# Banded local attention: the third and fourth group's query projections moved behind the value products and cut into runs of three or four parts

## The chip, the cores and the metric
The kernel runs on one core of one Trainium2 chip. The metric is the device time of one execution in microseconds (us); lower is better. The core has five engines that run their own instruction streams and meet only at semaphores: TensorE (PE: matrix products and transposes; PEld is its weight load), VectorE (DVE), ScalarE (ACT), GpSimd (POOL) and SyncE (SP, which issues the transfers).

## The reference
Four layers are computed on x of shape (1, 512, 1024) in float32. The change lies in the attention of the last but one part of the second block:

```python
q = (rmsnorm(h, b_pre_norm) @ b_w_q).reshape(bsz, s, 16, 64)      # 16 heads of 64
q = partial_rotary(q, cos, sin)
attn = sliding_window_sink_attention(q, k_sh, v_sh, b_sinks) @ b_w_o
# per block of 128 queries: keys of this block and of the one before, window 128
scores = jnp.where(valid, q @ k.T / 8, NEG)
probs = softmax(concat([scores, sink]))[..., :-1]
out = probs @ v
```

The 16 query heads share 4 key/value heads: 4 groups of 4 heads (KVH = 4, GROUP = 4), and the sequence has T = 4 blocks of 128, so there are 16 units of attention (UNITS), unit n being group g = n // 4 and block b = n % 4.

## The kernel before, in words
Every large product runs as three float32 products of a high and a low half (`mm3`, lines 1820 to 1822). The weights of each stage arrive in two buffers; ScalarE makes the high half (`split_high`, L743), GpSimd the low half (`low`, L639).

**The projection.** `queries(g, first, last)` projects the hidden state of all 512 tokens onto group g's 256 query columns: 16 parts of 3 matmuls each (two output tiles m, eight depths k), into PSUM banks 0 and 1. A call with `first == 0` waits for the split weights and for `q2_sin` of the group before last; the last part signals `used[g % 2]`. The group's result then goes: ScalarE copies it to `q2raw` (`raw_queries`, L1107), TensorE makes the partner rows (`partners`, L2324), VectorE multiplies them by the sine (L1802, signals `q2_sin`), GpSimd multiplies `q2raw` by the cosine (L627) and adds both (L630).

**A unit.** Unit n's work is spread over three engines:
- TensorE: `score2(n)` (4 heads, L2337), later `turn2(n)` (transposes of the probabilities, L2347; 4 or 8), later `weigh2(n)` (times the values, L2359; 4 or 8).
- VectorE: `top2(n)` (L1773 to L1778: window, maximum, sink), signals `m2_ready`; after ScalarE's exponentials `norm2(n)` (L1784 to L1787: sum, reciprocal, normalisation of the probabilities), signals `p2_ready`.
- ScalarE: `weigh2(n)` (exponentials, L1114 and L1116) and `turned2(n)` (transposed probabilities out of PSUM, L1125), `p2T_ready`.

`score2(n)` waits for `m2_ready` of unit n - 1. `turn2(n)` waits for `p2_ready` of unit n, that is for `norm2(n)`. VectorE's order in loop pass n is `top2(n + 1)`, in the passes with b == 1 the sine product of the next group and (from the second group on) `low_out` of the last one (L1791), and then `norm2(n)`.

**The order on TensorE** is written out by hand. The projections of groups 0 and 1 come ahead of the loop over the 16 units; those of groups 2 and 3 fill the units of groups 0 and 1. In loop pass n TensorE issues `score2(n + 2)`, a projection run in the passes with b == 1, `turn2(n)`, `weigh2(n - 1)`, and a projection run in the passes with b == 2 and 3. Each engine executes in order, so a wait in front of `turn2` holds all that follows.

After the 16 units come the output projection (`out_stage("wo")`) and the last feed-forward layer (`in_stage("gu1")`, `out_stage("dn1")`).

Of the kernel before, what the change touches and what calls it, by code (L numbers as in the profile page):

```python
# [17 lines left out]
K = D // P  # L18
# [17 lines left out]
HD, KVH, GROUP = 64, 4, 4  # L36
# [155 lines left out]
def program(nc, a, out):  # L192
    with ExitStack() as ctx:
# [1621 lines left out]
        def _(pe):  # L1815
            mm, tr = nc.tensor.matmul, nc.tensor.transpose

            def mm3(dst, lh, ll, rh, rl, first, last):

                mm(dst, lh, rh, start=first, stop=False, skip_group_check=True)  # L1820
                mm(dst, lh, rl, start=False, stop=False, skip_group_check=True)  # L1821
                return mm(dst, ll, rh, start=False, stop=last, skip_group_check=True)  # L1822

            def wcols(w, s):
                return w[s][:, :].rearrange("p (k n) -> p k n", n=256)
# [235 lines left out]
            for f in range(K):  # L2061
                g, m = f // 2, f % 2
# [243 lines left out]
            def queries(g, first, last, tok=slice(0, S)):  # L2306

                s = g % 2
                if first == 0:
                    pe.wait_ge(w_split[s], B.split[s] + g // 2 + 1)  # L2310
                    if g >= 2:
                        pe.wait_ge(q2_sin, g - 1)
                for j in range(first, last):
                    m, k = j // K, j % K
                    c = slice(m * P, (m + 1) * P)
                    ins = mm3(PS[:, m, tok], wcols(WH, s)[:, k, c], wcols(WL, s)[:, k, c], hH[:, k, tok], hL[:, k, tok], k == 0, k == K - 1)
                if last == 2 * K and tok.stop == S:
                    ins.then_inc(used[s], 1)

            def partners(g):  # L2320

                pe.wait_ge(q2_raw, g + 1)
                for m in range(2):
                    ins = mm(PS[:, m if g else 6 + m, :], turn_b, q2raw[:, m, :], start=True, stop=True)  # L2324
                ins.then_inc(q2_turn, 1)

            def score2(n):
                g, b = n // T, n % T
                if b == 0:
                    pe.wait_ge(q2_ready, g + 1)  # L2330
                if n:
                    pe.wait_ge(m2_ready, n)
                lo = max(b - 1, 0) * P
                for h in range(GROUP):
                    r = slice((h % 2) * HD, (h % 2 + 1) * HD)
                    c = (h // 2) * 2 * P
                    ins = mm(PS[:, 2 + h % 2, c + (0 if b else P):c + 2 * P], q2[g % 2][r, h // 2, b * P:(b + 1) * P],  # L2337
                             kdup[r, g, lo:(b + 1) * P], start=True, stop=True)
                ins.then_inc(s2_done, 1)

            def turn2(n):
                if n:
                    pe.wait_ge(p2T_ready, n)
                pe.wait_ge(p2_ready, n + 1)
                for h in range(GROUP):
                    for k in range(0 if n % T else 1, 2):
                        ins = tr(two(4)[:, 2 * h + k, :], p2[n % 3][:, h, k * P:(k + 1) * P], ident)  # L2347
                ins.then_inc(t2_done, 1)

            def weigh2(n):  # L2350
                g, b = n // T, n % T
                if b == 0 and g:
                    pe.wait_ge(o2_low, 2 * g)
                pe.wait_ge(p2T_ready, n + 1)
                ks = range(0 if b else 1, 2)
                c = (b % 2) * 2 * P
                for k in ks:
                    for o in range(2):
                        ins = mm(PS[o * HD:(o + 1) * HD, 6 + b // 2, c:c + 2 * P], vall[:, b - 1 + k, g * HD:(g + 1) * HD],  # L2359
                                 p2T[n % 2][:, 4 * o + k:4 * o + 4:2, :], start=(k == ks[0]), stop=(k == 1), skip_group_check=True)  # L2360
                ins.then_inc(pv2_done, 1)
# [13 lines left out]
            def ahead_wo(first, last):  # L2375

                for kt in range(first, last):
                    s, d = kt // 2, kt % 2
                    pe.wait_ge(w_split[s], BASE["wo"].split[s] + 1)
                    pe.wait_ge(o2_low, kt + 1)  # L2380
                    pe.wait_ge(q2_sin, KVH - 1)
                    out_tile(o2H, o2L, kt, s, d, 0, kt == 0, False)

            AHEAD = {UNITS - 3: (0, 1), UNITS - 2: (1, 2), UNITS - 1: (2, 4)}
            for n in range(UNITS):
                g, b = n // T, n % T
                if n + 2 < UNITS:
                    score2(n + 2)
                if n in AHEAD:
                    ahead_wo(*AHEAD[n])  # L2390
                if b == 0 and g + 1 < KVH:
                    partners(g + 1)
                if b == 1 and g + 2 < KVH:
                    queries(g + 2, 0, 5)
                turn2(n)
                if n:
                    weigh2(n - 1)
                if b >= 2 and g + 2 < KVH:
                    queries(g + 2, *((5, 10), (10, 2 * K))[b - 2])
            weigh2(UNITS - 1)  # L2400
            turn = turner("wo", 4, x_hat)
            out_stage("wo", o2H, o2L, lambda kt: pe.wait_ge(o2_low, kt + 1),
# [39 lines left out]
```

## Time and profile before

| | us |
|---|---|
| median of 3 runs | 1876.33 |
| lowest and highest of them | 1875.57, 1877.78 |
| the profiled execution, its own time | 1876.41 |
| its span (first to last instruction) | 1874.3 |
| TensorE busy | 1807.3 (96% of the span), 8798 matmuls |
| VectorE busy | 791.5 (42%) |
| ScalarE busy | 746.1 (40%) |
| GpSimd busy | 788.9 (42%) |

Times in the trace are microseconds from the start of the span. The 16 units and the projections in them lie at about 1359 to 1463 us. A row of the timeline is one instruction, or several alike merged (x8), with its start, its duration, and in brackets the idle time of the engine just before it and whose signal ended it. Matmuls overlap, so the time that a piece of work takes on TensorE is read from its start to the next start. The table by stretches gives the busy time of every engine and PEclk, the share of full clock granted to TensorE (1.00 is 2.4 GHz, 0.50 is 1.2 GHz).

### The profile page before, as it was taken

How to read it: one execution, taken by the hardware profiler on the slowest of the kernel's cores; microseconds unless marked ns; L12 is line 12 of the kernel's file. 1: busy time of each engine (PE TensorE's matmuls, PEld its weight loads, DVE VectorE, ACT ScalarE, POOL GpSimd, SP SyncE). 2: the span in 40 equal slices, each digit the busy share in tenths (PEclk: the TensorE clock that was granted, in tenths of full speed). 3: DMA queues.
4: the chain of work that ended last, by engine and by line, in shares of the span. 5: the costliest groups of instructions: out<-in, count | busy, mean ns of one | idle time of the engine just before them, and what ended most of it. 6: DMA issues, size and time to landing. Idle time of an engine off the chain costs nothing.

```text
span 1874.3 us, 24002 instructions
## 1 busy us (share of the span) xinstructions
PE 1807.3 (96%) x8798; PEld 1494.8 (80%) x8798; DVE 791.5 (42%) x1388; ACT 746.1 (40%) x1043; POOL 788.9 (42%) x992
## 2 busy tenths in 40 slices
PE   6999999989999999899999999999997999999998
PEld 6788878878788878788888888888965788888886
DVE  5775775367677632623241111103678341111102
ACT  3423331365656542322253344214456453443212
POOL 0375454354101162355335555443443135555351
PEclk9999999999999999999999999999999999999999
DMA  9543565221212132233233343232311133433321
GB/s 314 172 135 90 151 202 183 93 82 37 73 36 73 45 124 90 68 93 132 90 91 90 93 109 112 102 112 82 114 45 45 46 91 90 109 92 90 120 94 67
DMA packets 209320, 190.94 MB, mean 102 GB/s; under 512 B 10475, under 2 KB 189538, under 8 KB 209250
## 3 DMA queue, kind: packets, MB, share of 16 engines
q1 hardware_dynamic: 208608, 189.69, 32.7%
q8 instruction: 46, 0.75, 0.2%
q10 hardware_dynamic: 642, 0.29, 0.1%
q14 instruction: 24, 0.20, 0.0%
HBM read 187.86 MB, written 2.10 MB: 101 GB/s over the span
## 4 chain that ended last, share of the span: by engine, by line
PE 86%; DVE 5%; ACT 3%; POOL 3%; issue 2%; DMA 0%; SPq 0%; ACTq 0%; POOLq 0%; DVEq 0%
PE PS L1820 27%; PE PS L1822 26%; PE PS L1821 26%; POOL w_low L639 2%; PE PS L2168 1%; ACT w_high L743 1%; PE PS L1949 1%; PE PS L2199 1%; POOL w_low L677 1%; DMA ada_raw<-in_ada_w 0%; DVE soft L1775 0%; DVE probs L1773 0%; PE PS L2359 0%; PE PS L2191 0%; PE PS L2190 0%
## 5 line engine op out<-in xcount | busy, mean ns | idle before, releaser
L639 POOL TENSOR_TENSOR w_low<-w_raw,w_high 128x256 fp32r<-128x256 f32 x905 | 701.6, 811 | 841.2 <-ACT w_high L743 841.2
L1820 PE MATMUL PS<-h_high,w_high 128*128 128x512 f32 (+1 forms) x1488 | 560.7, 377 | 15.4 <-DVE h_low L1453 7.0
L1821 PE MATMUL PS<-h_low,w_high 128*128 128x512 f32 (+1 forms) x1488 | 553.7, 372 | 0.0
L1822 PE MATMUL PS<-h_high,w_low 128*128 128x512 f32 (+1 forms) x1488 | 553.6, 372 | 0.0
L743 ACT ACTIVATE w_high<-w_raw 128x2048 fp32r<-128x2048 f32 (+2 forms) x150 | 280.2, 1868 | 683.8 <-PE PS L1822 669.1
L1820 PEld LDWEIGHTS PS<-h_high,w_high 128*128 128x128 f32 x1488 | 281.6, 189 | 68.6 <-DVE h_low L1453 8.3
L1822 PEld LDWEIGHTS PS<-h_high,w_low 128*128 128x128 f32 x1488 | 281.5, 189 | 48.8
L1821 PEld LDWEIGHTS PS<-h_low,w_high 128*128 128x128 f32 x1488 | 281.8, 189 | 45.7 <-issue 0.7
L1363 DVE TENSOR_TENSOR gate_buf<-gate_buf,PS 128x512 f32<-128x512 f32 x44 | 30.3, 688 | 334.9 <-ACT gate_buf L876 334.3
L1183 DVE TENSOR_TENSOR w_low<-w_raw,w_high 128x2048 fp32r<-128x2048 f32 (+1 forms) x15 | 33.3, 2220 | 325.4 <-ACT w_high L743 325.4
L1820 PE MATMUL PS<-w_high,ff_high 128*128 128x512 f32 x352 | 137.2, 390 | 0.1
L1822 PE MATMUL PS<-w_high,ff_low 128*128 128x512 f32 x352 | 137.0, 389 | 0.0
L1821 PE MATMUL PS<-w_low,ff_high 128*128 128x512 f32 x352 | 137.0, 389 | 0.0
L667 POOL TENSOR_TENSOR w_low<-w_raw,w_high 128x256 fp32r<-128x256 f32 x35 | 29.8, 882 | 165.0 <-ACT w_high L743 165.0
L1820 PEld LDWEIGHTS PS<-w_high,ff_high 128*128 128x128 f32 x352 | 66.1, 188 | 14.6 <-POOL w_low L639 1.0
L1821 PEld LDWEIGHTS PS<-w_low,ff_high 128*128 128x128 f32 x352 | 66.1, 188 | 13.7
L1822 PEld LDWEIGHTS PS<-w_high,ff_low 128*128 128x128 f32 x352 | 66.1, 188 | 13.6
L1820 PE MATMUL PS<-w_high,o_high 128*128 128x512 f32 x192 | 75.5, 393 | 0.6 <-POOL w_low L639 0.6
L1821 PE MATMUL PS<-w_low,o_high 128*128 128x512 f32 x192 | 74.8, 389 | 0.0
L1822 PE MATMUL PS<-w_high,o_low 128*128 128x512 f32 x192 | 74.8, 389 | 0.0
L977 ACT ACTIVATE probs<-PS,soft 128x128 f32<-128x128 f32 (+1 forms) x64 | 33.8, 528 | 75.8 <-DVE soft L1573 75.8
L1367 DVE TENSOR_TENSOR ff_low<-gate_buf,ff_high 128x512 f32 x44 | 41.9, 953 | 40.8 <-ACT ff_high L880 40.8
(310 smaller groups left out, 2574.8 us busy)
## 6 DMA issues: line engine op xcount, KB each, us to landing
w_raw<-in_f_gate_up SPq DMA_DIRECT2D x88, 512.0 KB, 4.9
w_raw<-in_f_down SPq DMA_DIRECT2D x40, 512.0 KB, 4.3
w_raw<-in_e_w_in SPq DMA_DIRECT2D x32, 512.0 KB, 5.0
gains<-in_ada_w SPq DMA_DIRECT2D x16, 1024.0 KB, 5.2
w_raw<-in_a_w_in SPq DMA_DIRECT2D x24, 512.0 KB, 4.5
w_raw<-in_o_w_in SPq DMA_DIRECT2D x20, 512.0 KB, 4.3
ada_raw<-in_ada_w SPq DMA_DIRECT2D x8, 1024.0 KB, 13.3
w_raw<-in_e_w_out SPq DMA_DIRECT2D x16, 512.0 KB, 5.6
```

The costliest lines, as they stand in the source:

```text
L639: ins = nc.gpsimd.tensor_tensor(WL[s][:, piece], raw[s][:, piece], WH[s][:, piece].bitcast(F32), ALU.subtract)
L667: ins = nc.gpsimd.tensor_tensor(WL[1][:, piece], raw[1][:, piece], WH[1][:, piece].bitcast(F32), ALU.subtract)
L677: nc.gpsimd.tensor_tensor(WL[1][:, h:], raw[1][:, h:], WH[1][:, h:].bitcast(F32), ALU.subtract).then_inc(pool_half, 1)
L743: nact(WH[s][:, 0:n], raw[s][:, 0:n], ACT.Copy).then_inc(w_high[s], 1)
L977: nact(pm[u % 2][:, 0:w], PS[:, 2 + u % 2, 0:w], ACT.Exp, scale=MLA_SCALE, bias=soft[:, u % 2, 1, 0:1], accum_out=soft[:, u % 2, 2, 0:1]). ...
L1183: v.tensor_tensor(WL[s][:, 0:size], raw[s][:, 0:size], WH[s][:, 0:size].bitcast(F32), ALU.subtract).then_inc(w_split[s], 1)
L1363: v.tensor_tensor(buf[s][:, :], buf[s][:, :], PS[:, 2 * s + 1, :], ALU.mult).then_inc(prod_ready, 1)
L1367: v.tensor_tensor(lows[:, f, :], buf[s][:, :], fH[:, f, :].bitcast(F32), ALU.subtract).then_inc(gate_low, 1)
L1820: mm(dst, lh, rh, start=first, stop=False, skip_group_check=True)
L1821: mm(dst, lh, rl, start=False, stop=False, skip_group_check=True)
L1822: return mm(dst, ll, rh, start=False, stop=last, skip_group_check=True)
L1949: ins = tr(two(2 * t if b is None else b)[:, k, :], src[:, k * P:(k + 1) * P], ident)
```

## The change
The projections of groups 2 and 3 are the same 16 parts each, in the same order, in the same passes of the loop. Only where they stand in a pass, and the length of the runs, differ:

| pass | before | after |
|---|---|---|
| b = 1 | `queries(0, 5)`, `turn2`, `weigh2` | `turn2`, `weigh2`, `queries(0, 4)` |
| b = 2 | `turn2`, `weigh2`, `queries(5, 10)` | `queries(4, 7)`, `turn2`, `weigh2`, `queries(7, 10)` |
| b = 3 | `turn2`, `weigh2`, `queries(10, 16)` | `queries(10, 13)`, `turn2`, `weigh2`, `queries(13, 16)` |

```diff
                 if b == 0 and g + 1 < KVH:
                     partners(g + 1)
-                if b == 1 and g + 2 < KVH:
-                    queries(g + 2, 0, 5)
+                if b >= 2 and g + 2 < KVH:
+                    queries(g + 2, *((4, 7), (10, 13))[b - 2])
                 turn2(n)
                 if n:
                     weigh2(n - 1)
-                if b >= 2 and g + 2 < KVH:
-                    queries(g + 2, *((5, 10), (10, 2 * K))[b - 2])
+                if b and g + 2 < KVH:
+                    queries(g + 2, *((0, 4), (7, 10), (13, 2 * K))[b - 1])
             weigh2(UNITS - 1)
```

No instruction is added or removed, and no transfer is touched.

## Rows read from the trace of the kernel before

**Rows 1.** Who TensorE waited for, 1500 us to the end: total us, times, longest.
```profile
PE PS L1820 <- DVE h_low L1453: 0.7, 1, 0.7
```

**Rows 2.** Timeline of TensorE, units 1 to 3 (start us, us, engine line op).
```profile
1372.11 1.14 PE L2337 MATMUL PS<-k_dup,q 64*128 64x256 f32 x8 [0.59 <-DVE soft L1778]
1373.33 0.47 PE L1820 MATMUL PS<-h_high,w_high 128*128 128x512 f32 x1
...
1376.63 0.39 PE L1822 MATMUL PS<-h_high,w_low 128*128 128x512 f32 x1
1376.96 1.06 PE L2347 MATMUL PS<-small,probs 128*128 128x128 f32 x8
1377.96 0.65 PE L2359 MATMUL PS<-probs_t,v_all 128*64 128x256 f32 x4
1379.82 0.71 PE L2337 MATMUL PS<-k_dup,q 64*128 64x128 f32 x8 [1.21 <-DVE soft L1778]
1381.36 1.06 PE L2347 MATMUL PS<-small,probs 128*128 128x128 f32 x8 [0.82 <-DVE probs L1787]
1382.35 1.08 PE L2359 MATMUL PS<-probs_t,v_all 128*64 128x256 f32 x8
1383.37 0.50 PE L1820 MATMUL PS<-h_high,w_high 128*128 128x512 f32 x1
...
1387.01 1.13 PE L2337 MATMUL PS<-k_dup,q 64*128 64x256 f32 x8
...
1390.12 0.50 PE L1820 MATMUL PS<-h_high,w_high 128*128 128x512 f32 x1
...
1394.42 1.13 PE L2337 MATMUL PS<-k_dup,q 64*128 64x256 f32 x8
```

**Rows 3.** Timeline of VectorE, the same stretch: the normalisations of units 1 and 3.
```profile
1373.50 3.32 DVE L1787 TENSOR_TENSOR probs<-probs,soft 128x1024 f32<-128x1024 f32 x1
...
1385.54 1.51 DVE L1787 TENSOR_TENSOR probs<-probs,soft 128x1024 f32<-128x1024 f32 x1
```

**Rows 4.** Timeline of GpSimd, the same stretch.
```profile
1373.33 2.40 POOL L630 TENSOR_TENSOR q<-q,q_tmp 128x1024 f32<-128x1024 f32 x1 [1.84 <-DVE q_tmp L1802]
```

**Rows 5.** Timeline of TensorE, units 5 to 8.
```profile
1398.97 1.14 PE L2337 MATMUL PS<-k_dup,q 64*128 64x256 f32 x8
...
1403.88 1.06 PE L2347 MATMUL PS<-small,probs 128*128 128x128 f32 x8
...
1406.74 0.72 PE L2337 MATMUL PS<-k_dup,q 64*128 64x128 f32 x8 [1.22 <-DVE soft L1778]
1408.28 1.06 PE L2347 MATMUL PS<-small,probs 128*128 128x128 f32 x8 [0.82 <-DVE probs L1787]
...
1421.31 1.13 PE L2337 MATMUL PS<-k_dup,q 64*128 64x256 f32 x8
```

**Rows 6.** Timeline of VectorE, normalisation of unit 5 and `top2` of unit 10.
```profile
1402.50 1.22 DVE L1787 TENSOR_TENSOR probs<-probs,soft 128x1024 f32<-128x1024 f32 x1
...
1422.49 1.22 DVE L1773 TENSOR_TENSOR probs<-PS,swa 128x1024 f32<-128x1024 f32 x1 [3.45 <-PE PS L2337]
```

**Rows 7.** Timeline of TensorE, work that followed two of its longest waits.
```profile
279.84 0.35 PE L1835 MATMUL PS<-small,ada_acc 128*128 128x1 f32 x2 [3.74 <-DVE mod L1226]
...
1431.01 1.90 PE L2347 MATMUL PS<-small,probs 128*128 128x128 f32 x8 [4.02 <-DVE probs L1787]
1432.84 1.12 PE L2359 MATMUL PS<-probs_t,v_all 128*64 128x256 f32 x4
1433.90 0.98 PE L2337 MATMUL PS<-k_dup,q 64*128 64x128 f32 x8
```

**Rows 8.** Stretches: busy us (xcount) of PE, PEld, DVE, ACT, POOL, then PEclk.
```profile
280.70:284.10 3.40, 3.40 (x10) 2.73 (x9) 0.42 (x1) 0.00 (x0) 3.40 (x6) 0.51 0.78 302
...
1431.00:1434.50 3.50, 3.49 (x18) 2.41 (x20) 3.33 (x8) 1.55 (x2) 0.00 (x0) 0.51 0.00 0
1434.50:1438.00 3.50, 2.45 (x22) 1.52 (x20) 3.40 (x7) 3.50 (x11) 2.15 (x4) 1.00 0.00 0
```

## The prediction, made before the changed kernel was run

> **What bounds the kernel now.** I read the page's busy table first: TensorE is busy for 96% of the span (the small table of times), so time moves only if TensorE's waits or its own work move. The table of waits for the stretch after 1500 us comes next: its longest wait there is 0.7 us, once [rows 1]. Behind the attention TensorE runs without gaps, and a delay handed over at the end of the 16 units arrives whole at the end of the kernel. What is left is the timeline of TensorE in the passes that hold the moved projections, units 1 to 3 and units 5 to 7 [rows 2, 5], with the timelines of VectorE and GpSimd beside it, which say what ends each wait [rows 3, 4, 6].
>
> Two things are to be seen. Before `turn2(1)` TensorE shows no idle time, and yet it is VectorE that lets it go: the normalisation `norm2(1)` starts at 1373.50 and takes 3.32 us, to 1376.82 [rows 3], and `turn2(1)` starts at 1376.96 [rows 2]. The last projection matmul ahead of it started at 1376.63 and would have let the next one go about 0.3 us later [rows 2]. Projection and wait end together: five parts of projection cover the wait completely. The other two passes do show waits, 1.21 us before `score2(4)` and 0.82 us before `turn2(2)` [rows 2], which no projection covers.
>
> Group 1's units repeat it: `norm2(5)` ends at 1402.50 + 1.22 = 1403.72 [rows 6] and `turn2(5)` starts at 1403.88, with 1.22 and 0.82 us of waiting behind it [rows 5].
>
> **The change part by part.** Nothing is added or removed, so everything is a matter of what stands over which wait. No transfer and no queue of SyncE or GpSimd is passed; the moved instructions are matmuls only.
>
> *Prices.* A run of 15 matmuls with the step out of it takes 1387.01 - 1383.37 = 3.64 us, one of 18 takes 1394.42 - 1390.12 = 4.30 [rows 2]. Inside the first run 14 steps take 1376.63 - 1373.33 = 3.30, or 0.236 with the slow first step. With 0.23 per matmul a run costs about 0.2 us beyond its matmuls. The bounds: 0.1 (15 x 0.236 = 3.54 against 3.64) and 0.34 (three matmuls cost 0.66 by the difference of the two runs, so 15 cost 3.30). A run of four parts is then 12 x 0.23 + 0.2 = 2.96, one of three parts 9 x 0.23 + 0.2 = 2.27. Eight transposes take 1.00 to the next start (1376.96 to 1377.96), eight value products 1.02 (1382.35 to 1383.37), four 0.65 less an overlap of 0.07, or 0.58, eight short scores 0.71 less the same, or 0.65, long scores 1.13 less the same, or 1.07 [rows 2].
>
> *Pass 1, the run ahead of `turn2(1)` taken away.* `score2(3)` ends at 1372.11 + 1.14 = 1373.25 [rows 2]. What `norm2(1)` waits for is not TensorE's projection: it is ScalarE's exponentials, and then VectorE's own queue. `norm2(1)`'s last instruction begins at 1373.50 whatever TensorE does and lasts 3.32 us, since GpSimd's addition of 2.40 us began at 1373.33 [rows 4] and the same kind of instruction takes 1.22 us elsewhere [rows 6]. So `turn2(1)` starts at 1376.96 as before, and the 3.71 us from 1373.25 are now bare.
>
> The Trainium skill (SBUF — State Buffer, section Who interferes with whom) says that a VectorE instruction with two SBUF inputs and a GpSimd instruction that reads SBUF hold one shared read interface for a whole instruction each, and the later one blocks. The trace agrees (3.32 us beside 2.40 us). By that rule a shift of TensorE's work alone frees nothing here, so the sum stays the same.
>
> *From there on, unit by unit.* `turn2(1)` 1376.96; `weigh2(0)` 1377.96; projection of four parts 1378.54; `score2(4)` 1381.50 (VectorE had been ready since before 1379.82); three parts 1382.15; `turn2(2)` 1384.42 (ready since before 1381.36); `weigh2(1)` 1385.42; three parts 1386.44; `score2(5)` 1388.71; three parts 1389.78; `turn2(3)` 1392.05; `weigh2(2)`; after 1.00 + 1.02 three parts at 1394.07; `score2(6)` at 1396.34. Before it stood at 1394.42 [rows 2]: 1.9 us later. The two waits are covered (2.03 us won, and about 0.15 at the start of the old run), 3.71 are laid bare, and two more runs cost 0.4.
>
> Is anything late in between? `top2(4)` waits for `score2(4)`, which ends 1.7 us later than before; `norm2(3)` ended at 1385.54 + 1.51 = 1387.05 [rows 3] and would end before 1388.8, well ahead of `turn2(3)` at 1392.05. The weight buffers are released 1.9 us later, and nothing uses them at once.
>
> *Group 1's units.* All engines start this group from `score2(6)`, so `norm2(5)` moves by 1.9 too. TensorE is then free at 1398.97 + 1.9 + 1.14 = 1402.0 [rows 5] and must wait for 1403.88 + 1.9 = 1405.8: 3.8 us bare. From `turn2(5)` to `score2(10)` the walk is the same 19.4 us, where it was 1421.31 - 1403.88 = 17.4 [rows 5]. `score2(10)` is 3.9 us late in all. With the bounds for a run, 2 x 2 extra runs cost 0.4 to 1.4 instead of 0.8, so 3.5 to 4.5.
>
> *The clock.* The two bare waits of 3.7 and 3.8 us have a second price. After a wait of 4.02 us the transposes took 1.90 us instead of 1.06 [rows 7, 2], and the granted clock was 0.51, the 1.2 GHz level, from 1431.0 to 1434.5, and 1.00 again after it; after a wait of 3.74 us it was 0.51 from 280.7 to 284.1 [rows 7, 8]. The new waits have the length of the second. In the first case transposes and value products took 1433.90 - 1431.01 = 2.89 us where they take 1.58 at 2.4 GHz: 1.3 us lost by then, about 1.6 in the stretch. A stretch of 3.4 us that lies wholly on projections loses half, 1.7. One that begins before the wait ends loses less, and 0 is the bound if the clock stays up. I take 1.5 for each wait, near the rows, so 3.0.
>
> **Sum.** 1876.41 (the profiled execution) + 3.9 + 3.0 = 1883.3. That execution lies 0.08 us above the median, so the median after is 1883.2, which is 0.37% slower.
>
> **Rivals.**
> - *The clock stays at 2.4 GHz after one or both of the waits.* For it: the waits are somewhat shorter than 4.02 us. Against it: 3.74 was followed by 0.51. Price: 1880.2 for none, 1881.7 for one.
> - *The low clock stays for a second stretch.* The work that follows the wait begins with eight transposes of little load. Another 3.4 us at half the speed costs 1.7 for each wait: up to 1886.6. Against it: the same transposes and value products follow the 4.02 us wait, and PEclk reads 1.00 from 1434.50 on [rows 8]. The Trainium skill (TensorE: Matmul & The Clock Gate, Part 4: PE-mode transpose) says that transposes do not count as activity like products do, which would favour this rival. The trace does not bear it out after its one such burst.
> - *The other side: `turn2` is not held.* If `norm2(1)` and `norm2(5)` were ready when the scores end, both groups would win 2.03 + 0.15 us of covered waits less 0.4 for two runs, 3.6 in all: 1872.8, just inside "no change" as defined below. It breaks even where `turn2(1)` starts some 1.8 us after 1373.25, so with `norm2(1)` done by about 1374.9. Against it: even at 1.22 us and without GpSimd it would end at 1374.7, and in the second group, where it does take 1.22, it ends at 1403.72 with the scores done at 1400.1 [rows 5, 6].
> - *The delay is absorbed behind unit 8*, in the 4.02 us wait of unit 9: 1876.3. Against it: VectorE had itself been idle for 3.45 us until `score2(10)` let `top2(10)` go [rows 6]; the chain that makes the wait of unit 9 starts from the delayed instruction, and moves with it.
>
> **How the numbers follow.** "No change" means within 0.2%, 3.75 us, about what a measurement of this kernel can tell. The forecast, both waits bare and a low stretch after each, has 0.73. No or one low stretch has 0.16 (1880.2 to 1881.7), a second low stretch 0.04, `turn2` not held 0.03, absorbed 0.02, and 0.02 is left for what I don't see. The range takes the first two: from 1879.8 (extra runs at their lower bound, no low stretch) to 1885.3 (upper bound of the runs, 4.5, and 3.4 for the clock give 1884.2, with 1.1 for the scatter of the runs before). Slower by over 0.2% (above 1880.1): 0.73 + 0.04 and 0.13 of the 0.16, 0.90. Within 0.2%: 0.03 of the 0.16 with the two cases of 0.03 and 0.02, so 0.08. Faster: the 0.02 that is left.
>
> **What would show it.** In TensorE's timeline a wait of about 3.7 us for VectorE L1787 right after the score products near 1373, and another near 1402; no wait before the following `score2` and `turn2`; PEclk near 0.5 for some 3.4 us around 1377 and 1406. `score2(6)` 1.9 us later without the clock's share and about 3.4 with it, `score2(10)` 3.9 and about 6.9, and the same distance at the end. The prediction is wrong if `turn2(1)` starts before about 1375, if the clock reads 1.00 throughout both groups, or if the wait of unit 9 shrinks by what came in late.

## The result

| | before | changed |
|---|---|---|
| median (lowest, highest), 8 runs each | 1878.05 (1875.57, 1879.32) | 1883.20 (1881.39, 1885.21) |
| profiled execution, its own time | 1876.41 | 1882.92 |
| its span | 1874.3 | 1880.8 |

The ratio of the changed kernel to the one before is 1.0033, with an interval of 1.0024 to 1.0043: 0.33% or some 6 us slower (4.5 to 8); the two medians of the table lie 5.2 us apart. The direction, the size and both mechanisms came out as forecast. That the median fell on 1883.2 to the tenth is luck: with five more runs the kernel before has a median 1.7 us above the one that the sum started from. The like-for-like figure is that of the profiled executions, 6.5 us against 6.9 forecast. Part of that match is luck too: the two groups cost 0.8 us less than forecast, and 0.7 us that nobody forecast came in behind them.

The timeline of TensorE after the change, where [rows 2] and [rows 5] showed it before:

```profile
1371.77 1.13 PE L2337 MATMUL PS<-k_dup,q 64*128 64x256 f32 x8 [0.58 <-DVE soft L1778]
1376.56 1.94 PE L2347 MATMUL PS<-small,probs 128*128 128x128 f32 x8 [3.66 <-DVE probs L1787]
...
1382.43 0.71 PE L2337 MATMUL PS<-k_dup,q 64*128 64x128 f32 x8
...
1385.26 1.03 PE L2347 MATMUL PS<-small,probs 128*128 128x128 f32 x8
1386.22 1.08 PE L2359 MATMUL PS<-probs_t,v_all 128*64 128x256 f32 x8
...
1389.51 1.13 PE L2337 MATMUL PS<-k_dup,q 64*128 64x256 f32 x8
...
1397.02 1.13 PE L2337 MATMUL PS<-k_dup,q 64*128 64x256 f32 x8
...
1406.41 1.56 PE L2347 MATMUL PS<-small,probs 128*128 128x128 f32 x8 [3.71 <-DVE probs L1787]
...
1427.09 1.13 PE L2337 MATMUL PS<-k_dup,q 64*128 64x256 f32 x8
```

The 1.2 and 0.8 us waits of [rows 2, 5] are gone, and in their place stand two waits of 3.66 and 3.71 us, both for the normalisation of the unit that is to be transposed. The transposes behind them take 1.94 and 1.56 us instead of 1.06. VectorE, which sets the end of both waits, did in unit 1 what it did in [rows 3]. In unit 5 the last instruction of the normalisation takes 1.22 us and is late for another reason: the sine product starts at 1401.06, `low_out` follows it at 1402.81, after 0.53 us idle for ScalarE, and only then comes the normalisation.

```profile
1373.16 3.26 DVE L1787 TENSOR_TENSOR probs<-probs,soft 128x1024 f32<-128x1024 f32 x1
...
1402.81 1.23 DVE L1791 TENSOR_TENSOR o_low<-PS,o_high 128x1024 fp32r<-128x1024 f32 x1 [0.53 <-ACT o_high L1129]
```

The table by stretches (the columns of [rows 8]) shows the clock:

```profile
1371.80:1376.10 4.30, 1.10 (x8) 0.66 (x8) 4.23 (x4) 2.12 (x10) 2.34 (x1) 1.00 0.00 0
1376.10:1379.50 3.40, 2.94 (x13) 1.88 (x13) 3.26 (x8) 0.96 (x2) 0.00 (x0) 0.50 0.02 5
1379.50:1383.00 3.50, 3.50 (x22) 2.69 (x20) 1.28 (x2) 3.50 (x10) 1.56 (x3) 1.00 0.00 0
...
1406.80:1410.30 3.50, 3.50 (x14) 2.23 (x13) 3.33 (x8) 2.29 (x2) 0.00 (x0) 0.51 0.03 7
...
1437.50:1444.40 6.90, 6.00 (x32) 3.72 (x30) 6.62 (x14) 5.91 (x12) 3.45 (x6) 0.51 0.00 0
```

TensorE drops to the 1.2 GHz level about the end of each of the two new waits (at 1376.1, 0.4 us before the transposes start, and at 1406.8, 0.4 us after), and is back at 2.4 GHz some 3.4 us later. Where the time went, each part as a difference of two starts in one profile:

| | before | changed | difference |
|---|---|---|---|
| unit 3's scores to unit 6's | 1394.42 - 1372.11 = 22.31 | 1397.02 - 1371.77 = 25.25 | 2.94 |
| unit 6's scores to unit 10's | 1421.31 - 1394.42 = 26.89 | 1427.09 - 1397.02 = 30.07 | 3.18 |
| unit 10's scores to the end of the span | 452.99 | 453.71 | 0.72 |

The changed kernel's attention starts 0.34 us earlier, which the differences leave out: 2.94 + 3.18 + 0.72 - 0.34 = 6.5. Of the 0.72, 0.69 lie before the last value products (1466.97 in the changed profile), where the low stretch behind unit 9's wait lasts 6.8 us instead of 3.4 [rows 8]. Whether that is an effect of the change is not shown: the length of this stretch differs between two executions of one kernel too (last section).

### The profile page after: what moved, and what is told of

Its sections match the earlier page's. It is cut to its first block, busy times and chain, and to the rows that moved or that the text cites. A ratio compares the mean times of both kernels' runs of the same rounds, so it can differ in the third digit from the quotient of the medians.

```text
span 1880.8 us, 24002 instructions
## 1 busy us (share of the span) xinstructions
PE 1811.6 (96%) x8798; PEld 1496.9 (80%) x8798; DVE 791.4 (42%) x1388; ACT 746.7 (40%) x1043; POOL 787.4 (42%) x992
## 4 chain that ended last, share of the span: by engine, by line
PE 87%; DVE 5%; ACT 3%; POOL 3%; issue 2%; DMA 0%; SPq 0%; ACTq 0%; POOLq 0%; DVEq 0%
PE PS L1820 27%; PE PS L1821 26%; PE PS L1822 26%; POOL w_low L639 2%; PE PS L2168 1%; ACT w_high L743 1%; PE PS L1949 1%; PE PS L2199 1%; POOL w_low L677 1%; PE PS L2359 1%; PE PS L2347 1%; DMA ada_raw<-in_ada_w 0%; PE PS L2191 0%; PE PS L2190 0%; DVE probs L1579 0%
```

## The experiments

The measure used throughout beside the timed ratio is **S**, the time on TensorE from the start of unit 3's scores (about 1372) to that of unit 10's in each kernel's profile. It holds all that the change moves, and leaves out what differs elsewhere, the low stretch behind unit 9's wait above all. S is 49.20 us before and 55.32 after the change.

| kernel | ratio to before (interval) | runs | S, us | first and second wait before turn2, us |
|---|---|---|---|---|
| changed | 1.0033 (1.0024 to 1.0043) | 8 | 55.32 | 3.66, 3.71 |
| changed, second job | 1.0031 (1.0019 to 1.0043) | 6 | 55.47 | 3.65, 3.71 |
| first run ahead again | 0.9997 (0.9988 to 1.0006) | 11 | 49.18 | 0.63, 0.81 |
| only the first run moved | 1.0043 (1.0029 to 1.0057) | 5 | 54.99 | 3.65, 3.71 |
| the same, second job | 1.0036 (1.0023 to 1.0050) | 5 | 54.96 | 3.65, 3.72 |
| first run issued twice | 1.0015 (1.0005 to 1.0024) | 11 | 52.53 | 0.64, 0.82 |
| first run split 2 and 3 | 1.0007 (0.9998 to 1.0016) | 11 | 50.89 | 1.99, 2.16 |
| norm first | 0.9986 (0.9977 to 0.9995) | 11 | 46.97 | 0.49, none |
| norm first, groups 0 and 1 | 0.9988 (0.9979 to 0.9997) | 11 | 46.97 | 0.49, none |
| norm first, old order | 0.9995 (0.9986 to 1.0004) | 11 | 50.04 | none (1.63, 2.61 before the run) |
| norm first, three runs | 0.9996 (0.9987 to 1.0005) | 11 | 47.68 | 0.49, none (1.39 before turn2(6)) |

**The first run ahead again.** All else stays as changed.

```diff
-                if b >= 2 and g + 2 < KVH:
-                    queries(g + 2, *((4, 7), (10, 13))[b - 2])
+                if b and g + 2 < KVH:
+                    queries(g + 2, *((0, 4), (4, 7), (10, 13))[b - 1])
                 turn2(n)
                 if n:
                     weigh2(n - 1)
-                if b and g + 2 < KVH:
-                    queries(g + 2, *((0, 4), (7, 10), (13, 2 * K))[b - 1])
+                if b >= 2 and g + 2 < KVH:
+                    queries(g + 2, *((7, 10), (13, 2 * K))[b - 2])
```

> The changed kernel, but with the run of four parts of pass 1 put ahead of the transposes again (0 to 4 ahead of turn2 in the passes with b = 1; the rest as changed, so five runs per group). Bare-wait theory: turn2(1) starts where it did before, the four parts (2.96 us) cover most of the 3.7 us, the wait left is some 0.7 us and the clock stays up. score2(4) waits about 1.2 us again, the wait before turn2(2) stays covered, two more runs cost 0.4 us. By the walk each group ends 0.24 us later than before: 0.5 us slower than the kernel before, that is between -0.5 and +1.5. Rival (the cost is in cutting the projection into short runs, or in where the later runs stand): this kernel keeps both, so it stays 4 us or more slower than before.

The ratio is 0.9997, and S is 49.18, that of the kernel before to 0.02 us. In its timeline the wait is down to 0.63 us and the transposes take 1.06:

```profile
1376.77 1.06 PE L2347 MATMUL PS<-small,probs 128*128 128x128 f32 x8 [0.63 <-DVE probs L1787]
```

The cost of the change is in the place of the first run. The five short runs alone cost nothing that shows; they win the 0.8 us wait and pay it back.

**Only the first run moved.** The other half of the pair, and its repetition in a second job beside the changed kernel.

```diff
-                if b == 1 and g + 2 < KVH:
-                    queries(g + 2, 0, 5)
                 turn2(n)
                 if n:
                     weigh2(n - 1)
-                if b >= 2 and g + 2 < KVH:
-                    queries(g + 2, *((5, 10), (10, 2 * K))[b - 2])
+                if b and g + 2 < KVH:
+                    queries(g + 2, *((0, 5), (5, 10), (10, 2 * K))[b - 1])
```

> The kernel before, with nothing changed but the run of five parts in the passes with b = 1, which goes behind the value products (three runs of 5, 5 and 6 parts). Bare-wait theory: waits of 3.7 us for VectorE L1787 before turn2(1) and turn2(5), the waits of 1.2 and 0.8 us covered, no extra runs: 1.5 us later per group, 3.0 in all, and 1.3 to 1.7 us for each of two stretches at 1.2 GHz, so 6 us slower than before (4.5 to 6.5), some 0.8 less than the whole change. Rival (short runs are the cost): close to before, within 1 us.

> The changed kernel itself, run beside the next one on the same chip. Its first timing gave 1.0033 (1.0024 to 1.0043) of the kernel before; expected again 5 to 6.5 us slower than before.

> The kernel before with only the first run moved behind the value products, as once before (three runs per group, not five). Its first timing, five runs, came out 7.5 us over the kernel before, where the walk with the clock gave 6, and above the changed kernel, where the walk gave 0.8 us below it. In its profile the stretch from unit 3's scores to unit 10's was 0.3 us shorter than the changed kernel's. Theory (short runs cost some 0.1 to 0.2 us each, the rest was scatter): equal to the changed kernel within its interval, or up to 0.8 us below. Rival (something in this order costs 1.5 us or more that the walk does not see): again 1.5 us or more above the changed kernel.

The first timing was 1.0043, over the 6.5 us expected as the most and above the changed kernel's 1.0033. The second gave 1.0036 beside 1.0031 for the changed kernel on the same chip, and the intervals overlap nearly whole. The rival of an unseen 1.5 us is not borne out: in the profiles S is 54.99 and 54.96, 0.3 to 0.5 us under that of the changed kernel. So the four extra runs cost about 0.1 us each, if the low stretches cost the same in both kernels; they do not lie on quite the same work (the transposes of unit 5 take 1.56 us in the one and 1.27 in the other). The timings alone don't resolve that half microsecond.

**The first run issued twice.** Once ahead of `turn2`, and once more where the change has it. The second issue starts the sums anew, so the result is that of the second and the first is pure filler.

```diff
-                if b >= 2 and g + 2 < KVH:
-                    queries(g + 2, *((4, 7), (10, 13))[b - 2])
+                if b and g + 2 < KVH:
+                    queries(g + 2, *((0, 4), (4, 7), (10, 13))[b - 1])
                 turn2(n)
```

> The changed kernel with its run of four parts issued twice in the passes with b = 1: once ahead of turn2 and again, starting the sum anew, behind weigh2. 24 matmuls more than the changed kernel, 2.96 us of extra work per group, lying wholly in the bare wait of 3.7 us. Theory of two prices: the wait itself stays hidden work, so the 3.9 us of the walk stay, but the clock no longer falls at turn2(1) and turn2(5), which gives back 1.3 to 1.7 us each: 2.5 to 3.4 us faster than the changed kernel although it does more, 3.9 us (3.4 to 4.5) slower than the kernel before. Rival (the clock falls anyway, or its fall costs nothing because others are waited for): as slow as the changed kernel, 5 to 7 us over before. Rival (TensorE's work is the bound there): 6 us slower than the changed kernel.

24 matmuls more, and some 0.17% (3 us) faster than the changed kernel (1.0015 against 1.0031 and 1.0033). The intervals of these timings still overlap a little; the profile leaves no doubt, S falls by 2.8 us. The same stretch that stood at PEclk 0.50 is at 1.00:

```profile
1376.70:1380.20 3.50, 3.48 (x20) 2.64 (x21) 3.33 (x8) 2.38 (x2) 0.00 (x0) 1.00 0.00 0
1405.30:1408.80 3.50, 3.50 (x20) 2.63 (x21) 3.33 (x8) 2.40 (x2) 0.00 (x0) 1.00 0.02 7
```

This separates the two prices. The clock costs 55.32 - 52.53 = 2.8 us, 1.4 for each stretch (1.5 forecast). The wait that nothing useful covers, net of what it wins elsewhere, costs 52.53 - 49.20 = 3.3 us (3.9 forecast).

**The first run split.** Two parts ahead of `turn2`, three behind `weigh2`.

```diff
                 if b == 1 and g + 2 < KVH:
-                    queries(g + 2, 0, 5)
+                    queries(g + 2, 0, 2)
                 turn2(n)
                 if n:
                     weigh2(n - 1)
-                if b >= 2 and g + 2 < KVH:
-                    queries(g + 2, *((5, 10), (10, 2 * K))[b - 2])
+                if b and g + 2 < KVH:
+                    queries(g + 2, *((2, 5), (5, 10), (10, 2 * K))[b - 1])
```

> The kernel before, its run of five parts in the passes with b = 1 split: two parts stay ahead of turn2, three go behind weigh2. Bare-wait theory: two parts cover 1.6 us of the 3.7, 2.0 us stay bare; the three parts cover the 1.2 us wait before score2(4) and the 0.8 us one before turn2(2), one extra run of 0.2 us per group: by the walk 0.1 to 0.2 us later per group, so within 0.5 us of the kernel before if the clock stays up, and up to 3.4 us more if a wait of 2.0 us makes it fall too. Rival (any projection behind the value products costs, however short the wait): 2 us or more slower with the clock up.

The ratio is 1.0007, not to be told from no change. The profile is worth more than the time:

```profile
1376.90 1.06 PE L2347 MATMUL PS<-small,probs 128*128 128x128 f32 x8 [1.99 <-DVE probs L1787]
...
1403.89 1.94 PE L2347 MATMUL PS<-small,probs 128*128 128x128 f32 x8 [2.16 <-DVE probs L1787]
```

```profile
1376.90:1380.30 3.40, 3.40 (x20) 2.55 (x21) 3.23 (x8) 2.30 (x2) 0.00 (x0) 1.00 0.00 0
1403.70:1407.10 3.40, 3.21 (x13) 2.16 (x14) 3.23 (x9) 1.24 (x2) 0.00 (x0) 0.50 0.01 2
```

After the wait of 1.99 us the clock stayed up, after the one of 2.16 it fell. S is 50.89, 1.7 us over before: 0.1 of it in the group where the clock stayed up, 1.6 in the other. That is one low stretch, and next to nothing for the waits themselves. Two microseconds of bare wait break even with the 2.0 us won behind, which is where the walk in the prediction puts the balance.

**Norm first.** The changed kernel, with VectorE's order in the passes with b = 1 turned round.

```diff
-                if b == 1 and g + 1 < KVH:
-                    dve.wait_ge(q2_turn, g + 2)
-                    dve.wait_ge(q2_ready, g + 1)
-                    v.tensor_tensor(q2tmp[:, :, :], PS[:, 0:2, :], sin2, ALU.mult).then_inc(q2_sin, 1)
+                norm2(n2)
                 if b == 1 and g:
                     low_out(g - 1)
-                norm2(n2)
+                if b == 1 and g + 1 < KVH:
+                    dve.wait_ge(q2_turn, g + 2)
+                    dve.wait_ge(q2_ready, g + 1)
+                    v.tensor_tensor(q2tmp[:, :, :], PS[:, 0:2, :], sin2, ALU.mult).then_inc(q2_sin, 1)
```

> The changed kernel with VectorE's order altered: in the passes with b = 1 norm2 goes first, then low_out, then the sine product of the next group. The theory says that turn2(1) waits for VectorE's sine product (1.2 us) and for GpSimd's addition that this product lets go (2.2 us of the 3.3 us of norm2's last instruction). With norm2 ahead of both, turn2(1) should start about 3.1 us earlier (a wait of about 0.6 us left), the same at turn2(5), with no fall of the clock in either; unit 9's wait of 4.0 us should shrink to about 1 or be split. By the walk 1.2 us faster than before per group and 1 to 2 us in group 2: 3 to 5 us faster than the kernel before, 8 to 11 faster than the changed one. Rival (turn2(1) waits for the exponentials or for its own operand, not for VectorE's queue): as slow as the changed kernel.

0.14% faster than the kernel before (0.05 to 0.23%), some 2.6 us, a little under the 3 to 5 us expected, and 8.9 us under the changed kernel's median. On VectorE:

```profile
1373.18 1.22 DVE L1787 TENSOR_TENSOR probs<-probs,soft 128x1024 f32<-128x1024 f32 x1
1374.33 1.22 DVE L1805 TENSOR_TENSOR q_tmp<-PS,swa 128x1024 f32<-128x1024 f32 x1
```

and on TensorE, with unit 3's scores at 1372.93:

```profile
1374.55 1.06 PE L2347 MATMUL PS<-small,probs 128*128 128x128 f32 x8 [0.49 <-DVE probs L1787]
...
1431.49 0.71 PE L2337 MATMUL PS<-k_dup,q 64*128 64x128 f32 x8 [3.86 <-DVE soft L1778]
```

The normalisation takes 1.22 us where it took 3.3, since GpSimd's addition now starts behind it, and the transposes wait 0.49 us instead of 3.66. This shows that the long wait came from what VectorE did before the normalisation. Which part took how much is read from the rows: in unit 1 the sine product in front (1.22 us) and GpSimd's addition beside (3.26 us instead of 1.22), in unit 5 the sine product and `low_out` in front. The first two groups gain 2.2 us over the kernel before. The third group gained nothing, against what was expected (39.7 us from unit 10's scores to the last value products, 39.2 before): unit 9's wait of 4.0 us is gone from `turn2(9)`, but one of 3.86 us stands before `score2(12)`, which waits for `top2(11)`. VectorE has the same work to do there, and TensorE has no projection left to fill in.

**Norm first in the first two groups only.**

```diff
+                if b == 1 and g < 2:
+                    norm2(n2)
+                    if g:
+                        low_out(g - 1)
+                    dve.wait_ge(q2_turn, g + 2)
+                    dve.wait_ge(q2_ready, g + 1)
+                    v.tensor_tensor(q2tmp[:, :, :], PS[:, 0:2, :], sin2, ALU.mult).then_inc(q2_sin, 1)
+                    continue
                 if b == 1 and g + 1 < KVH:
```

> The changed order of TensorE, with VectorE's norm2 ahead of low_out and of the sine product in pass b = 1 of the first two groups only; in the third group VectorE keeps its old order. With norm2 first everywhere, the first two groups took 46.97 us from unit 3's scores to unit 10's (before: 49.20), but the rest up to the last value products took 39.7 instead of 39.2. Theory: the sum of the two good parts, 0.5 us less than with norm2 first everywhere, 3 to 3.5 us faster than the kernel before. Rival (the last part's 0.5 us came from the clock and not from VectorE's order): the same as with norm2 first everywhere.

0.9988 against 0.9986: no gain from it, and its profile shows two stretches at 1.2 GHz, near 1430 and 1440, and 40.1 us from unit 10's scores to the last value products (1420.07 to 1460.13), not 39.2. So the rival is borne out: with VectorE's old order in the third group the half microsecond did not come back, and more time at the low clock stands there than in the kernel before. What sets the number of low stretches is not shown.

**Norm first with TensorE's old order, and with three runs.** The same edit of VectorE, once on the kernel before and once on the kernel with only the first run moved.

> TensorE's order of the kernel before (five parts ahead of turn2 in the passes with b = 1) with VectorE's norm2 ahead of low_out and the sine product. The run ahead of turn2 starts only when the sine product is done, since it overwrites the banks that the product reads. Theory: the two orders need each other. By the walk the run starts 1.6 us later in group 0 and 2.7 us later in group 1 and holds turn2 behind it; with the 1.2 and 0.8 us waits covered by that delay the two groups end 0.5 us earlier and 0.4 us later than before: 49.0 us from unit 3's scores to unit 10's, within 0.5 us of the kernel before there. Rival (VectorE's order alone is the gain): about 47 us there and 3 us faster than before, as with the changed order of TensorE.

> norm2 first on VectorE, and on TensorE three runs per group (5, 5 and 6 parts), all behind the value products. Theory: as good as the five runs of the change with norm2 first, since the waits left there are short: four runs fewer at 0.1 us each, 46.6 us from unit 3's scores to unit 10's, 2.5 to 3.3 us faster than before. Rival (the short runs of the change cover a wait that the long ones leave open): 1 us or more slower than with the five runs.

With the old order the gain is gone (0.9995, S 50.04). The run ahead of `turn2` overwrites the banks that the sine product reads, so it waits 1.63 and 2.61 us for it, and holds the transposes, which start only at 1380.58 and 1407.66:

```profile
1375.67 0.77 PE L1820 MATMUL PS<-h_high,w_high 128*128 128x512 f32 x1 [1.63 <-DVE q_tmp L1805]
...
1404.15 0.47 PE L1820 MATMUL PS<-h_high,w_high 128*128 128x512 f32 x1 [2.61 <-DVE q_tmp L1805]
```

S came out 1.0 us over the 49.0 expected, with the clock low behind the first of these waits. The longer of the two waits is not followed by a low stretch:

```profile
1375.60:1378.70 3.10, 3.02 (x7) 2.47 (x8) 2.93 (x8) 0.00 (x0) 2.38 (x1) 0.51 0.03 5
1404.10:1407.50 3.40, 3.35 (x15) 2.81 (x16) 3.23 (x8) 0.00 (x0) 2.40 (x1) 1.00 0.00 0
```

The two orders need each other, as expected; it is S that shows it (50.04 against 46.97), since the intervals of the timings (0.9995 and 0.9986) overlap. With three runs S is 47.68 where 46.6 was expected, and here the rival is right in kind: a 1.39 us wait for `norm2(6)` before `turn2(6)` appears, which the change's short run ahead of `turn2` covers. The timed ratio, 0.9996 (0.7 us faster than before, where 2.5 to 3.3 were expected), has an interval that overlaps that of the five runs. So by the profiles the change's short runs are worth 0.7 us of S once `norm2` goes first, and nothing before.

## Why the prediction was right

- *What sets `turn2(1)` and `turn2(5)`.* Right: the wait was forecast as 3.7 and 3.8 us and measured as 3.66 and 3.71. That no idle time showed there before [rows 2] did not mean that the projection set the pace; putting the run back removed the cost (S 49.18 against 49.20), and the norm-first kernel showed VectorE's order as the cause. One part of the account is off: the prediction names ScalarE's exponentials first among what `norm2(1)` waits for. In the norm-first kernel `norm2(1)` follows directly behind `top2(2)`, with no idle time on VectorE, so they had been ready; only VectorE's queue held it.
- *What it wins.* Right: the two later waits vanished in both groups.
- *The extra runs.* The term was mis-sized. 0.2 us for each was taken, between bounds of 0.1 and 0.34, and about 0.1 was measured (S of the changed kernel less that with three runs, 0.33 and 0.51 us in two pairs of profiles, over four runs). In the changed timeline the run ahead of `turn2(2)` makes `score2(4)` to `weigh2(1)` last 1386.22 - 1382.43 = 3.79 us, where it lasts 1384.36 - 1382.69 = 1.67 in the profile with only the first run moved, which has no run there: 2.12 for nine matmuls, 0.05 over 9 x 0.23. The same run behind the value products costs what was forecast: 1389.51 - 1386.22 = 3.29, less 1.02 for the value products, is 2.27. The step that was priced goes with the place of a run, and the extra runs of the change stand in the cheap one. That accounts for most of 3.9 against 3.3 us.
- *The clock.* Right in kind, and 1.4 us each instead of 1.5, shown by the filler kernel. The argument from the length of the wait is weaker than it looked: 1.63 us was followed by the low level and 2.61 us was not, in one execution.
- *No absorption behind unit 8.* Right; unit 9's wait is 4.01 us as before. Not foreseen was that the low stretch behind it would last twice as long in the changed profile, 0.7 us more. Without it the two profiles would lie 5.8 us apart.
- *The rivals.* A second low stretch in a row, favoured by what the Trainium skill says of transposes (TensorE: Matmul & The Clock Gate, Part 4: PE-mode transpose), did not come after either of the new waits. In the third group, behind its long wait, it did: in 8 of the 12 profiles of this case the low level lasts 6.8 or 10.2 us there, where a single stretch lasts 3.4. The argument against the rival, PEclk 1.00 from 1434.50 on, rested on one execution. No projection stands there and further waits follow, so the runs do not tell whether the transposes are the reason. `turn2` not held fell by the timeline. The sum was 6.9; the profiles give 2.9 + 3.2 + 0.7 - 0.3 = 6.5.

## What to carry to other kernels

Work that shows no idle time behind it may be the very cover of a wait: compare the start of the next instruction with the end of its releaser on the other engine before moving the work away. Here both ended within a quarter of a microsecond, and 3.7 us came to light. A bare wait on TensorE cost its length, less what the moved work won elsewhere, and 1.4 us more where the clock fell about its end; even useless matmuls in it gave that back. And look at what the other engine does ahead of the awaited instruction: turning round three instructions of VectorE took the reason for the wait away, and only then did the new order pay.

## What the runs showed of the hardware

- The clock's answer to a wait does not go by the wait's length alone. In the kernel with the first run split 1.99 us was followed by 1.00 and 2.16 us by 0.50; with `norm2` first and TensorE's old order 1.63 us was followed by 0.51 and 2.61 us by 1.00, each pair in one execution.
- The same wait is not always followed by the same low stretch. That of 4.0 us in unit 9 was followed by 3.4 us at the low level in the kernel before, by 6.8 us in both profiles of the changed one, and by 10.2 and 6.8 us in the two profiles of the kernel with only the first run moved.
- Single executions of one kernel scatter by 4 us: the kernel before ran from 1875.15 to 1879.26 in 27 runs of one job, with 14 of them at or below 1877.24, 13 at or above 1878.50, and none between; in another job seven of 22 runs lie in that gap. The time goes with the granted clock of the run: its mean over the span was 0.993 to 0.996 in the 14 quicker runs and 0.991 or 0.993 in the 13 others. So how the low stretches fall may be the reason, but only one execution of the kernel before was profiled, so it stays open.
